# Gate columns, context updates and the mixing product between the last slab's groups, and two mixers' transposes behind the recurrence

## The reference

```
h = x * (1 + sc1) + sh1;  hc = ctx * (1 + sc1c) + sh1c      # 1024 tokens, 256 context tokens
z = h @ w_in
y_a = mlstm_mixer(...)   # 4 heads of 64, both directions; the state starts from the context
y_b = sgu_mixer(...)     # layer norm, a 128x128 mixing product per group, u * (mixed + b_s)
y_c = conv_mixer(...)    # gated depthwise convolution, layer norm, silu
y_d = s5_mixer(...)
y = concatenate([y_a, y_b, y_c, y_d]) @ w_out
x = layer_norm(ALPHA * x + g1 * y)
```

## Time and profile before

| | us |
|---|---|
| median of 3 runs | 2263.49 (2262.19 to 2265.18) |
| the profiled execution | 2257.96 |
| its span | 2256.2 |
| PE busy | 2104.8 (93%) |
| DVE, ACT, POOL busy | 1262.5, 746.2, 432.4 |
| mean granted clock of TensorE | 0.951 of full speed |

### The profile page before, as it was taken

How to read it: one execution, slowest core, us unless ns; L and a number is a source line. 1 busy time by engine, 2 the same in 40 slices (tenths; PEclk the granted TensorE clock), 3 DMA queues, 4 the chain that set the end, 5 groups by cost and what they waited for, 6 DMA issues and landing times. The chain is left out here.

```text
span 2256.2 us, 27762 instructions
## 1 busy us (share of the span) xinstructions
PE 2104.8 (93%) x10549; PEld 1589.7 (70%) x10549; DVE 1262.5 (56%) x2133; ACT 746.2 (33%) x1380; POOL 432.4 (19%) x472
## 2 busy tenths in 40 slices
PE   6998999996969999999999999899999887989998
PEld 4744464485758888888888887765888764658876
DVE  6581795247873333223544323568999777762433
ACT  2222021144113322222444222456222243761415
POOL 2900001042310000000000000323666551300210
PEclk9999999955989999999999999899999998999999
DMA  8543110023233333235343332212211102003101
GB/s 324 157 136 109 39 57 1 1 76 122 64 107 92 93 93 97 84 96 158 117 120 112 91 99 85 76 48 57 71 47 51 36 1 76 1 30 133 44 1 75
DMA packets 195977, 184.83 MB, mean 82 GB/s; under 512 B 13246, under 2 KB 166142, under 8 KB 192538
## 3 DMA queue, kind: packets, MB, share of 16 engines
q1 hardware_dynamic: 192890, 172.85, 24.6%
q0 software_dynamic: 2880, 10.49, 1.3%
q10 hardware_dynamic: 96, 0.02, 0.0%
HBM read 169.37 MB, written 12.64 MB: 81 GB/s over the span
## 5 line engine op out<-in xcount | busy, mean ns | idle before, releaser
L1835 DVE TENSOR_TENSOR ff_part<-ff_raw,ff_part 128x1024 fp32r<-128x1024 f32 (+2 forms) x152 | 164.9, 1085 | 435.8 <-ACT ff_part L1743 435.8
L1743 ACT ACTIVATE ff_part<-ff_raw 128x1024 fp32r<-128x1024 f32 (+2 forms) x152 | 144.0, 948 | 433.7 <-PE ps L1633 431.7
L1631 PE MATMUL ps<-h,ff_part 128*128 128x512 f32 x704 | 275.8, 392 | 4.2 <-DVE ff_part L1835 4.2
L1632 PE MATMUL ps<-h,ff_part 128*128 128x512 f32 x704 | 275.0, 391 | 0.0
L1633 PE MATMUL ps<-h,ff_part 128*128 128x512 f32 x704 | 274.9, 390 | 0.0
L2451 DVE TENSOR_SCALAR_CACHE_REDUCE pj_junk<-NM,prm 128x384 uint8<-128x384 f32 (+1 forms) x186 | 163.7, 943 | 1.1
L1631 PEld LDWEIGHTS ps<-h,ff_part 128*128 128x128 f32 x704 | 132.8, 189 | 31.9 <-DVE ff_part L1835 4.6
L1631 PE MATMUL ps<-pj_part,h 128*128 128x512 f32 x384 | 153.1, 399 | 0.2 <-ACT PJ L2308 0.2
L1633 PEld LDWEIGHTS ps<-h,ff_part 128*128 128x128 f32 x704 | 132.8, 189 | 27.9
L1632 PEld LDWEIGHTS ps<-h,ff_part 128*128 128x128 f32 x704 | 132.9, 189 | 27.4
L1632 PE MATMUL ps<-pj_part,h 128*128 128x512 f32 x384 | 150.3, 392 | 0.0
(11 more groups left out here) (595 smaller groups left out, 4023.1 us busy)
## 6 DMA issues: line engine op xcount, KB each, us to landing
ff_raw<-in_w_ffn_in SPq DMA_DIRECT2D x88, 512.0 KB, 3.7
s_wm<-in_w_mod SPq DMA_DIRECT2D x16, 1024.0 KB, 4.9
pj_raw<-in_w_in SPq DMA_DIRECT2D x64, 256.0 KB, 2.6
ff_raw<-in_w_ffn_out SPq DMA_DIRECT2D x32, 384.0 KB, 3.4
ff_raw<-in_w_ffn_out SPq DMA_DIRECT2D x32, 320.0 KB, 3.0
mod_w<-in_w_mod SPq DMA_DIRECT2D x8, 1024.0 KB, 9.3
mod_x<-in_x SPq DMA_DIRECT2D x8, 512.0 KB, 14.5
mx_spread<-mx_lfd SPq DMA_DIRECT2D x16, 256.0 KB, 3.4
```

Of the source, the lines that this page charges most:

```text
L1631: nc.tensor.matmul(out, w[0], x[0], start=first, stop=False)
L1632: nc.tensor.matmul(out, w[0], x[1], start=False, stop=False)
L1743: nc.scalar.activation(part[s % 2][0][:, 0:n, :], raw[s][:, 0:n, :], ACT.Copy).then_inc(hi, 1)
L1835: v.tensor_tensor(part[s % 2][1][:, 0:n, :], raw[s][:, 0:n, :], part[s % 2][0][:, 0:n, :].bitcast(F32), ALU.subtract).then_inc(lo, 1)
```

## The change

- `last_slab` sets the order of slab 3's chunks: 0, 1, 2, 9, 3, 8, 4, 7, 5, 6, that is in the order in which the two directions need them.
- On PE the gate columns come after the fifth group; the four context updates after the sixth, each into a bank of its own (`grown`); the mixing product after the seventh; then three groups and at once the scores of the first token step. The wait of the gate columns for `bdone` is gone, since DVE now combines the mixing product (`gates`) at the first token step, and the first two `scores` wait for it.
- ACT takes its exponentials after five read-outs and not seven, and the first two `weights` before the last two read-outs.
- `ke` has four buffers and not two, and POOL makes the first four keys as soon as the columns are there.
- SP reads the first six `spread` buffers back when `ga` is there, not when all groups are through; the buffers lie elsewhere.
- The 32 transposes of `yc` and `zb` come behind the recurrence, before those of `H`, in other banks; ACT reads them out behind its last `carried` and before `wo_split`.

```diff
+    last_slab = [0, 1] + [c for n in range(NT // 2) for c in (NCT + n, NL - 1 - n)]
+    def grown(n):
+        return K.bank[n if n < 2 * NCT else 4 * steps[n][1]]
...
-            sp.wait_ge(S["mm"], total)
+            sp.wait_ge(S["ga"], 1)
             for m in range(2 * NT):
...
+                if m == EARLY:
+                    sp.wait_ge(S["mm"], total)
...
-                if n >= 2:
-                    pool.wait_ge(S["umm"], n - 1)
+                if n >= 4:
+                    pool.wait_ge(S["umm"], n - 3)
+                pool.wait_ge(S["ev"], int(first[3]) + (2 if n < 4 else min(n - 1, NL)))
...
             n = slab(3, n, range(2, 5))
-            pe.wait_ge(S["sgn"], 1)
-            for g in range(4):
-                nc.tensor.matmul(K.bank[g][:].rearrange("p (i n) -> p i n", i=NT), K.wsT[:, g, :],
-                                 zb[:, :, W + g * HD:W + (g + 1) * HD], start=True, stop=True).then_inc(S["bmm"], 1)
-            n = slab(3, n, range(5, loads[3] - 1))
-            pe.wait_ge(S["ev"], total - 2)
-            pe.wait_ge(S["bdone"], 4)
+            pe.wait_ge(S["ev"], n - 2)
             pe.wait_ge(S["gb"], 1)
             for q in range(2 * NL):
...
             last.then_inc(S["colmm"], 1)
-            n = slab(3, n, range(loads[3] - 1, loads[3]))
-            pe.wait_ge(S["colev"], 1)
-            pe.wait_ge(S["ycn"], 1)
...
-            pe.wait_ge(S["yc_ev"], 4)
-            pe.wait_ge(S["yb_ev"], 4)
+            n = slab(3, n, range(5, 6))
...
+            pe.wait_ge(S["colev"], 1)
+            for m in range(2 * NCT):
+                update(m)
+            n = slab(3, n, range(6, 7))
+            pe.wait_ge(S["sgn"], 1)
+            pe.wait_ge(S["st"], 2 * NCT)
+            for g in range(4):
+                nc.tensor.matmul(K.bank[g][:].rearrange("p (i n) -> p i n", i=NT), K.wsT[:, g, :],
+                                 zb[:, :, W + g * HD:W + (g + 1) * HD], start=True, stop=True).then_inc(S["bmm"], 1)
+            n = slab(3, n, range(7, loads[3]))
+            scores(2 * NCT)
+            for n in range(2 * NCT, len(steps)):
                 update(n)
                 if n + 1 < len(steps):
                     scores(n + 1)
                 values(n)
+            pe.wait_ge(S["qn"], 2 * NT)
+            pe.wait_ge(S["ycn"], 1)
+            for q, b in enumerate((0, 4, 1, 2)):
...
+            for q, b in enumerate((5, 6, 0, 4)):
...
+            pe.wait_ge(S["yc_ev"], 4)
...
-            n = slab(3, n, range(7))
+            n = slab(3, n, range(5))
             act.wait_ge(S["ga"], 1)
...
-            n = slab(3, n, range(7, loads[3]))
+            n = slab(3, n, range(5, 8))
...
             act.wait_ge(S["colev"], 1)
+            act.wait_ge(S["sor"], 1)
             weights(0)
             weights(1)
+            n = slab(3, n, range(8, loads[3]))
             for m in range(2 * NT):
                 carried(m)
                 weights(m + 2)
...
```

More of the change, by code:

```diff
@@ L898, in stage_mixers @@
     flatps = K.ps[:].rearrange("p b c -> p (b c)")
-    decay = [K.bank[5][:, 0:2 * NL], K.bank[4][:, 3 * P + QS:3 * P + QS + 2 * NL]]
+    def grown(n):
+        return K.bank[n if n < 2 * NCT else 4 * steps[n][1]]
+    decay = [K.bank[d][:, 3 * P + QS:3 * P + QS + 2 * NL] for d in range(2)]
     with nc.Block() as block:
@@ L995, in gather @@
                 pool.wait_ge(S["hadd"], lat + 1)
-            keys(0)
-            keys(1)
+            for n in range(4):
+                keys(n)
+            for m in range(4):
+                hide(m)
             for n, (step, d) in enumerate(steps):
                 lat = n - 2 * NCT
-                if n + 2 < len(steps):
+                if 4 <= n + 2 < len(steps):
                     keys(n + 2)
-                if n == 0:
-                    for m in range(4):
-                        hide(m)
                 if lat >= 0:
@@ L1131, in update @@
                     o = (h // 2) * HX
-                    last = nc.tensor.matmul(K.bank[4 * d][(h % 2) * HD:(h % 2 + 1) * HD, o:o + HX], ke[d][:, h, :], vx[:, order[d][step], h, :],
+                    last = nc.tensor.matmul(grown(n)[(h % 2) * HD:(h % 2 + 1) * HD, o:o + HX], ke[n % 4][:, h, :], vx[:, order[d][step], h, :],
                                             start=True, stop=True)
@@ L1152, in _ @@
                 values(n)
+            pe.wait_ge(S["qn"], 2 * NT)
+            pe.wait_ge(S["ycn"], 1)
+            for q, b in enumerate((0, 4, 1, 2)):
+                for r in range(4):
+                    last = nc.tensor.transpose(K.bank[b][:, r * P:(r + 1) * P], yc[:, 4 * (q % 2) + r, (q // 2) * P:(q // 2 + 1) * P], K.ident[:])
+                last.then_inc(S["yc_tr"], 1)
+            for q, b in enumerate((5, 6, 0, 4)):
+                if q >= 2:
+                    pe.wait_ge(S["yc_ev"], q - 1)
+                for r in range(4):
+                    last = nc.tensor.transpose(K.bank[b][:, r * P:(r + 1) * P], zb[:, 4 * (q % 2) + r, (q // 2) * P:(q // 2 + 1) * P], K.ident[:])
+                last.then_inc(S["yb_tr"], 1)
+            pe.wait_ge(S["yc_ev"], 4)
             for q in (0, 2, 1, 3):
@@ L1155, in _ @@
                 for r in range(4):
-                    last = nc.tensor.transpose(K.bank[q][:, r * P:(r + 1) * P],
+                    last = nc.tensor.transpose(K.bank[(3, 1, 7, 2)[q]][:, r * P:(r + 1) * P],
                                                H[:, 4 * (q % 2) + r, 2 * (q // 2):2 * (q // 2) + 2, :], K.ident[:])
@@ L1179, in slab @@
                     else:
-                        take(kn[:, r, :], b[:, 0:W], last=False)
-                        take(vx[:, r, :, 0:HD], b[:, W:].rearrange("p (h e) -> p h e", h=HEADS))
+                        take(kn[:, last_slab[r], :], b[:, 0:W], last=False)
+                        take(vx[:, last_slab[r], :, 0:HD], b[:, W:].rearrange("p (h e) -> p h e", h=HEADS))
                     n += 1
@@ L1247, in _ @@
                 weights(m + 2)
+            for q, b in enumerate((0, 4, 1, 2)):
+                act.wait_ge(S["yc_tr"], q + 1)
+                nc.scalar.activation(K.yT[4 + q // 2][:, (q % 2) * HALF:(q % 2 + 1) * HALF], K.bank[b][:], ACT.Copy).then_inc(S["yc_ev"], 1)
+            for q, b in enumerate((5, 6, 0, 4)):
+                act.wait_ge(S["yb_tr"], q + 1)
+                nc.scalar.activation(K.yT[2 + q // 2][:, (q % 2) * HALF:(q % 2 + 1) * HALF], K.bank[b][:], ACT.Copy).then_inc(S["yb_ev"], 1)
             def wo_split(k):
@@ L1351, in _ @@
                 link(v.tensor_tensor_scan(lf[r, way[d]], d0[r, way[d]], ig[r, way[d]], LOW, ALU.add, ALU.max))
[L1353 to L1357, removed]
             link(v.memset(BE[0:QR, :], 0.0))
@@ L1400, in _, with gates @@
             dve.sem_inc(S["colev"], 1)
+            def gates():
+                for g in range(4):
+                    dve.wait_ge(S["bmm"], g + 1)
+                    o = zb[:, :, g * HD:(g + 1) * HD]
+                    v.scalar_tensor_tensor(out=o, in0=K.bank[g][:].rearrange("p (i n) -> p i n", i=NT), scalar=bs[:, g:g + 1], in1=o,
+                                           op0=ALU.add, op1=ALU.mult).then_inc(S["bdone"], 1)
             def finish(lat):
@@ L1416, in _ @@
                 c, lat = order[d][step], n - 2 * NCT
+                if lat == 0:
+                    gates()
                 if lat >= 0:
@@ L1423, in _ @@
                 if step < NL - 1:
+                    if 2 <= n < 2 * NCT:
+                        dve.wait_ge(S["st"], n - 1)
                     dve.wait_ge(S["umm"], n + 1)
```

40 lines of the change are left out of this document (13 added, 27 removed).

## The result

The changed kernel takes 2238.51 us (median of 4 executions, 2233.03 to 2240.72) against 2262.84 before (4 executions, 2260.68 to 2265.18): a ratio of 0.9889, 95% interval 0.9866 to 0.9911, so 24.3 us less. The forecast was 2242. The profiled execution took 2233.03, its span is 2231.2.

The account below looks back on a forecast made before the run. PE was taken to bound the recurrence, only through its halved clock. Start 1.2 later, recurrence 22.1 saved, tail 0.3 gained: -21.2 us from 2257.96 gives 2236.8, plus 5.5 for the median 2242.3; 8-in-10 range 2237 to 2268.

Parts of the forecast that it names:

- PE bounds the recurrence by its clock: Recurrence: PE sets its 4.4 us step only because idle time before it dropped the clock to 1.2 GHz.
- A new standstill of 4.8 us: Before the gate columns: PE waits 4.8 us for ACT's exponentials, which come behind the fifth read-out.
- The low clock behind it costs 5 us: Gate columns and next group: PE runs at 1.2 GHz after the standstill, costing 5 us, ends 1.5 and 8.
- The clock holds through the recurrence: Recurrence: it starts at 2.4 GHz and stays there; the likeliest case, chance 0.50.
- 3.0 us a step: Recurrence at full clock: DVE sets the step, 3.0 us with ends 2.7 and 3.6, where it was 4.4.
- POOL's blocks of DVE: Recurrence: POOL's work delays DVE operations, so the step is taken as 3.0 us against DVE's 2.67 of work.
- 22.1 us saved from the first scores to the readout: First scores to DVE's readout: 49.8 us instead of 71.9, so 22.1 saved.
- Behind the recurrence: 0.3 gained: After the recurrence: moved transposes and read-outs fit before w_out lands, 4.9 us after issue; nothing or 0.3 us gained.
- The sum: Whole kernel: 1.2 - 22.1 - 0.3 = -21.2 us, profiled execution 2236.8, median 5.5 us above it, 2242.3.
- Rival 1: Recurrence: the clock falls part way and can't come back, 2263 us if after 10 us; chance 0.30.

Follow-up runs that it names:

- e3: Kernel before the change, plus five unused products in PE's waits ahead of the first, third and fourth context updates; 2232.1 us.
- e6: Kernel before the change, plus only two unused products, in PE's wait ahead of the fourth context update; 2231.72 us.
- e5: Changed kernel with all sixteen spread reads held until slab 3's last group; seven executions 2244.16 to 2247.43 us, five 2267.7 to 2273.98.
- e2: Changed kernel with five unused products filling PE's wait for the exponentials before the gate columns; 2230.48 us.
- e8: e1 plus, behind the recurrence, the square root's table loaded early and the root taken before the splits of w_out; 2223.06 us.
- e1: Changed kernel with ACT's exponentials behind the fourth read-out of the last slab instead of the fifth; 2225.05 us.
- e9: e5 with eight unused products filling PE's wait before the first scores; 2243.64 us.
- e4: Changed kernel with the 32 transposes and their eight read-outs put back between the last group and the first scores; 2241.21 us.

## Why the prediction came out right, step by step

- *PE bounds the recurrence by its clock; the idle time before it took the clock, and the new order has none there.* Right, and shown from both sides: e3 and e6 give the gain without the change, e5 loses it in five of twelve executions with the change.
- *A new standstill of 4.8 us, released by the exponentials.* Right: 4.68.
- *The low clock behind it costs 5 us, ends 1.5 and 8.* Too little: the profile has 7.4 by its rows (columns 4.6, group 2.8), and e2 gave 7.2 in its profile and 8.0 in the medians. The clock came back only inside the group behind the columns, after 424 to 429 at 0.50, where I had let it return at the group's start; both cases of the earlier trace rows had shorter stretches. With it the scores start 3.5 us later than before, not 1.2.
- *The clock holds through the recurrence* (chance 0.50 of this case). Right, in every execution of the changed kernel: its spread is 7.7 us, and a lost clock costs 25.
- *3.0 us a step, ends 2.7 and 3.6.* This is the term with the largest error: 2.46 to 2.52, below the low end. That DVE sets the step was right. Two readings were off. PE's own step isn't half of 4.4 but 2.46: 4.43 / 2.46 = 1.8, so halving a duration of the slow clock gives too little, and PE is only 0.06 us short of being the bound. And I had added 0.33 us for POOL's blocks of DVE, which did not grow. L1410, now L1430, had 0.48 us and has 0.16 in most steps; POOL's mask now lies beside L1433, which takes 0.55 us and took 0.42:

```profile
481.65 0.64 POOL L995 TENSOR_SCALAR_AFFINE_SELECT mx_spread<-mx_spread 128x512 f32<-128x512 f32 x1
```

  The mask ends at 482.29 and L1433 at 482.57, 0.28 us later; where the same mask meets the 4-element L1430 (473.72, 0.63 us, mask until 474.33) that ends 0.02 us after it. So the block is still there, but L1433 starts when only 0.27 us of the mask are left, and pays 0.13 us. In the kernel before, the mask ended at 506.81, and L1410, started at 506.35 with 0.46 us of it left, paid 0.31. In all three the instruction ends as if its last 0.02 us (own time 0.16) or 0.28 us (own time 0.42) had to follow the mask. The price goes by how much of the mask is left at the start, and not by the size of the instruction. The Trainium skill ("SBUF — State Buffer", section "Who interferes with whom") has a DVE instruction with two SBUF inputs contend with a GpSimd instruction that reads SBUF; by that rule, the trace agrees. No run here tried it by itself.
- *22.1 us saved from the first scores to the readout.* 29.1, for the step: 13 x 0.5 = 6.5 of the 7.0 that were missing.
- *Behind the recurrence: 0.3 gained.* 0.6 lost. ACT was free before `w_out` landed, as said, but the transfer landed 5.9 us after its issue (506.25, to 512.19) and not 4.9. DVE's readout started 2.8 us behind the issue, where it had been 2.4 (532.32, to 534.69), so 0.4 of that 1.1 was made up and 0.6 was lost. e8 shows the wait on the path: taking it away in e1, where it was 1.76, gave 1.5 in the profiles and 2.0 in the medians. Why the transfer took longer stays open.
- *The sum.* -21.2 forecast, -24.9 in the profile: the step gave 7.0 more, the clock 2.3 and the tail 0.9 less. The forecast was closer than its terms were, and that is luck: errors of 7.0 one way and 3.2 the other. So is the last step of the sum. The median lay 5.5 us above the profiled execution in both kernels, but in four executions that spread over 7.7 us it might have been another.
- *Rival 1 rests on "it can't come back there".* The reason was wrong: in e5 it came back, under these very products. The rival didn't occur.

What the moves themselves are worth is seen with the clock equal: the kernel before with two products takes 2231.72, the change without its standstill 2225.05: 6.7 us, and 7.6 in the profiles of the stretch. As it was written, with the standstill, the change is slower than the kernel before with two products in its idle time, by 6.8 us in the medians and 4.0 in the profiles. How the gain of the moves divides is known for the transposes (2.7 to 3.9) and the early reads (5.1 to 8.0) only in the changed kernel, and not for the updates and the mixing product by themselves.

## What to carry to other kernels

Look at the granted clock before you count work: of the stretches at 1.2 GHz, find the idle time of TensorE in front of each, and ask whether another operation, or in the worst case a few unused products, fills it. Here two unused products, 2.0 us, gained 31 us. When you move work between engines, look at the engine that releases TensorE next: the same exponentials, one read-out earlier, were worth 12 to 13.5 us. And don't halve the durations of narrow products to get those at the full clock; look for a row at that clock.

## What the runs showed of the hardware

- Narrow fp32 products (64x65 to 128x128, weight loads 90% of the time) hold 2.4 GHz for 40 us once they start at it, with PE busy 37.90 of 38.80 us. The kernel before, busy 64.00 of 64 us with the same ones, stayed at 1.2 GHz.
- After a fall, the clock came back within 4 us of such work in some executions of one kernel (e5) and, by their times, not in others; of the kernel before, all executions beside these runs took 2256.66 to 2265.87 us, so none of them shows a return worth 25 us. What decides it stays open.
- Waits of 1.22, 0.58 and 0.76 us inside such work (e6), and of 0.85 (e9) and 1.22 us (e4) right before it, didn't take the clock; those of 2.67 us (with two short ones ahead of it), 4.68 and 7.45 us did.
- One wait of 0.90 us, at the end of the same recurrence, kept the clock in the changed kernel and in e9 and was followed by a fall in e1, e2, e5, e6 and e8, at its end or up to 1.4 us behind it. No rule by the length of a wait alone fits these runs.
